# Differential attention, opening: the update of x after the preceding layer norm on GpSimd instead of VectorE

## What is computed

```
# layer 0 ends:
x = layer_norm(ALPHA * x + (1 + gate2) * mlp(h), ln_g, ln_b)
# layer 1 (differential attention) begins:
h = x * (1 + scale1) + shift1
y = diff_attention(h)
x = layer_norm(ALPHA * x + (1 + gate1) * y, ln_g', ln_b')

def layer_norm(x, g, b):
    return (x - mean(x)) * rsqrt(var(x) + eps) * g + b
```

## Time and profile before

| | before |
|---|---|
| median of 3 executions | 1206.44 us (1204.35 to 1206.61) |
| the profiled execution: its time | 1205.25 us |
| the profiled execution: its span | 1203.1 us |
| TensorE busy | 1190.4 us, 99% of the span |
| VectorE busy | 951.6 us, 79% |
| ScalarE busy | 622.0 us, 52% |
| GpSimd busy | 116.9 us, 10% |
| mean granted TensorE clock | 0.998 |

### The profile page before, as it was taken

The page is one execution under the profiler, slowest core; times in us unless marked ns, Lnnn a source line. Parts: engine busy times, 40 slices in busy tenths (PEclk is TensorE's granted clock), DMA queues, the critical chain, the costliest instruction groups (busy, mean ns, idle before and its releaser), DMA issues.

```text
span 1203.1 us, 14725 instructions
## 1 busy us (share of the span) xinstructions
PE 1190.4 (99%) x5734; PEld 976.7 (81%) x5734; DVE 951.6 (79%) x1382; ACT 622.0 (52%) x851; POOL 116.9 (10%) x173
## 2 busy tenths in 40 slices
PE   9999999999999999999999999999999999999997
PEld 7888888888778888888887778888887788888885
DVE  7799868877766689888786668898998878775656
ACT  7445346465774463334465657443446576643441
POOL 2110130221300010000001100000101110000000
PEclk9999999999999999999999999999999999999999
DMA  9999996874655489989467537788857564566540
GB/s 317 336 344 323 311 297 190 286 250 160 178 178 173 152 294 353 311 313 327 162 220 242 162 115 274 269 304 276 313 190 251 165 224 140 177 223 212 191 160 35
DMA packets 148373, 282.71 MB, mean 235 GB/s; under 512 B 6976, under 2 KB 77072, under 8 KB 148304
## 3 DMA queue, kind: packets, MB, share of 16 engines
q1 hardware_dynamic: 127568, 209.73, 52.0%
q0 software_dynamic: 20576, 71.96, 17.9%
q10 hardware_dynamic: 160, 0.07, 0.0%
HBM read 274.61 MB, written 7.13 MB: 234 GB/s over the span
## 4 chain that ended last, share of the span: by engine, by line
PE 92%; DVE 3%; ACT 2%; issue 2%; DMA 0%; SPq 0%; DVEq 0%
PE ps L534 24%; PE ps L536 24%; PE ps L535 24%; PE ps L867 7%; PE ps L866 3%; PE ps L786 2%; PE ps L734 1%; ACT hi_w L1190 1%; PE ps L613 1%; PE ps L1077 1%; PE ps L740 1%; PE ps L1054 1%; PE ps L1056 1%; PE ps L943 1%; ACT area L1507 1%
## 5 line engine op out<-in xcount | busy, mean ns | idle before, releaser
L1706 DVE TENSOR_TENSOR lo_w<-w_raw,hi_w 128x2048 fp32r<-128x2048 f32 x194 | 440.7, 2286 | 61.2 <-ACT hi_w L1190 60.8
L1190 ACT ACTIVATE hi_w<-w_raw 128x2048 fp32r<-128x2048 f32 x195 | 370.0, 1915 | 55.6 <-DMA w_raw<-in_ffn_w_in 20.2
L534 PE MATMUL ps<-hi_w,xT 128*128 128x512 f32 x848 | 338.6, 399 | 0.0
L536 PE MATMUL ps<-lo_w,xT 128*128 128x512 f32 x848 | 330.9, 390 | 0.0
L535 PE MATMUL ps<-hi_w,xT 128*128 128x512 f32 x848 | 330.4, 390 | 0.0
L534 PEld LDWEIGHTS ps<-hi_w,xT 128*128 128x128 f32 x848 | 159.4, 188 | 36.3 <-issue 4.9
L534 PE MATMUL ps<-hi_w,hT_hi 128*128 128x512 f32 x480 | 188.3, 392 | 0.0
L536 PEld LDWEIGHTS ps<-lo_w,xT 128*128 128x128 f32 x848 | 159.2, 188 | 34.3
L536 PE MATMUL ps<-lo_w,hT_hi 128*128 128x512 f32 x480 | 187.0, 389 | 0.0
L535 PE MATMUL ps<-hi_w,hT_lo 128*128 128x512 f32 x480 | 186.8, 389 | 0.0
L535 PEld LDWEIGHTS ps<-hi_w,xT 128*128 128x128 f32 x848 | 159.5, 188 | 30.9
(11 more groups left out here) (324 smaller groups left out, 1169.9 us busy)
## 6 DMA issues: line engine op xcount, KB each, us to landing
w_raw<-in_ffn_w_in SPq DMA_DIRECT2D x86, 512.0 KB
aux<-in_ada_w POOLq DMA_DIRECT2D x34, 1024.0 KB, 7.1
w_raw<-in_mlp_w_up SPq DMA_DIRECT2D x32, 1024.0 KB
w_raw<-in_mlp_w_down SPq DMA_DIRECT2D x32, 1024.0 KB
w_raw<-in_w_mix_in SPq DMA_DIRECT2D x26, 1024.0 KB
w_raw<-in_ffn_w_out SPq DMA_DIRECT2D x22, 1024.0 KB
area<-in_ada_w POOLq DMA_DIRECT2D x14, 1024.0 KB, 6.1
w_raw<-in_moba_w_in SPq DMA_DIRECT2D x12, 1024.0 KB
```

The source lines that it names most:

```text
L534: pe.matmul(dst, lhs_hi, rhs_hi, start=start, stop=False)
L536: return pe.matmul(dst, lhs_hi, rhs_lo, start=False, stop=stop)
L1190: act.activation(hi_w[:, ring_slot(u), :], w_raw[:, ring_slot(u), :], ACT.Copy).then_inc(w_hi, 1)
L1706: vec.tensor_tensor(lo_w[:, ring_slot(u), :], w_raw[:, ring_slot(u), :], hi_w[:, ring_slot(u), :].bitcast(F32), ALU.subtract).then_inc(w_l ...
```

## The change

VectorE's two calls of `x_update` in differential attention go. GpSimd makes x instead, after it has issued the three row loads of the first MLP's layer norm and ahead of the head exchange: it waits for the rows, then for each tile until ScalarE has written its norm, multiplies by g and adds b, both over 1024 columns. VectorE gets three waits on `x_new`: ahead of the copy of turned keys over tile 0 (`heads_out(1)`), ahead of the transpose over tile 1 (`rotate(2)`), and ahead of the first use of x in the attention's own layer norm. The other calls of `x_update`, for the stages S_MOBA and S_DIFF, stay on VectorE.

```diff
-            def ln_summed(t, h):
+            def ln_summed(s, t, h):
                 z = zt[:, t, half_cols(h)]
                 steps.wait(vec)
+                if s == S_DIFF and (t, h) == (0, 0):
+                    vec.wait_ge(x_new, 2 * NT)
...
                     if n in (0, 2):
                         vec.wait_ge(rot_done, hb + 2 + n + 1)
+                        if diff and n == 2:
+                            vec.wait_ge(x_new, 2 * NT)
                         vec.transpose(late_turned[n // 2], buf.rearrange("p t n -> p (t n)")).then_inc(head_turned, 1)
...
                     vec.wait_ge(headT, hb // 2 + n // 2 + 1)
+                    if diff and n == 1:
+                        vec.wait_ge(x_new, NT + 1)
                     vec.tensor_copy(k2T[n // 2], bank(0, 2).rearrange("p (c n) -> p c n", c=4)).then_inc(headT_out, 1)
...
-                    if diff and slot == 6:
-                        x_update(S_MLP1, 1)
...
-                    if slot == 2 and diff:
-                        x_update(S_MLP1, 0)
...
                 if s == S_MLP1:
+                    pool.wait_ge(ld_row, 16 * 3 * (n + 2))
+                    for t in range(NT):
+                        pool.wait_ge(z_quarter, quarter(S_MLP1 - S_MOBA, t, 1))
+                        pool.tensor_tensor(x[:, t, :], zt[:, t, :], row_g, ALU.mult).then_inc(x_scaled, 1)
+                        pool.wait_ge(x_scaled, t + 1)
+                        pool.tensor_tensor(x[:, t, :], x[:, t, :], row_b, ALU.add).then_inc(x_new, 1)
                     heads_exchanged(6, late_turned[0], late_queries[0])
```

More of the change, by code:

```diff
@@ L324, in two_blocks_kernel @@
         ch_act, ch_lo = sem("ch_act"), sem("ch_lo")
-        x_new = sem("x_new")
+        x_new, x_scaled = sem("x_new"), sem("x_scaled")
         xsq_done, rstd_x_done = sem("xsq_done"), sem("rstd_x_done")
@@ L1859, in ln_stats, with ln_moments @@
                 steps.inc(vec.bn_stats(bst[:, t, h, :], zt[:, t, half_cols(h)]))
-            def ln_moments(t, h):
-                ln_summed(t, h)
+            def ln_moments(s, t, h):
+                ln_summed(s, t, h)
                 ln_stats(t, h)
@@ L1881, in ln_part @@
                 ln_gated(s, t, h)
-                ln_moments(t, h)
+                ln_moments(s, t, h)
             def ln_finish(t):
@@ L1907, in after_ln @@
                     vec.wait_ge(third_part_taken, LATE.index(b) + 1)
-                    ln_moments(1, 0)
+                    ln_moments(s, 1, 0)
                     ln_gated(s, 1, 1)
                     late_split(b, 0, 0, 0)
-                    ln_summed(1, 1)
+                    ln_summed(s, 1, 1)
                     late_split(b, 0, 0, 1)
@@ L1926, in after_ln @@
                     quarter_split(b, 0, 1)
-                    ln_moments(1, 1)
+                    ln_moments(s, 1, 1)
                     ln_variance(s, 1)
```

## The result

| kernel | median | lowest to highest | runs |
|---|---|---|---|
| before | 1206.53 us | 1204.35 to 1207.64 | 6 |
| with the change | 1210.92 us | 1209.48 to 1212.73 | 6 |

The ratio is 1.0039, with a 95% interval from 1.0027 to 1.0051: slower by 0.4%, 4.4 us. The prediction said 1210.8 us. The profiled execution with the change took 1209.55 us, with a span of 1207.6 us (before: 1205.25 and 1203.1).

What follows compares the result with a forecast made beforehand. TensorE, busy 1190.4 of 1203.1 us, was taken as the bound. Terms: +5.7 (entry) - 0.9 (keys' gap) - 0.4 (scores' gap) = +4.4 us; on the median of 1206.44, 1210.8 us, range 1207.8 to 1214.2.

Steps and rivals of the forecast that it cites:

- The entry: At the stage's entry GpSimd's instructions hold VectorE's, so TensorE's products come late: +3.1 us first tile, +5.7 us by the second.
- The price of 1024 columns: Each added GpSimd instruction of 128x1024 takes 2.4 us, between 2.26 and 2.56 us.
- Casts: VectorE's casts at the entry wait for GpSimd's whole instruction, like two-operand work; +4.4 us in all, without this +3.6.
- Rival 1: At the entry VectorE's casts are not held by GpSimd: +3.6 us, 1210.0 us; chance 0.12.
- The second tile's sequence: Second tile's entry: cast waits for GpSimd's product until 915.5, subtraction for its addition until 918.05; TensorE 5.7 us later.
- Rival 2: TensorE's clock falls in the entry's two new 3.3 us gaps: +5.8 us, 1212.2, up to 1214 us; chance 0.21.
- The keys' gap: TensorE's 0.90 us wait before the keys' transposes at 933.32 closes: -0.9 us.
- The scores' gap: TensorE's 0.44 us wait for the head exchange before the scores at 940.32 closes: -0.4 us.
- Rival 3: At the entry GpSimd gives way to VectorE, so nothing is late: 0 us, 1206.4 us; chance 0.15.
- Rival 4: GpSimd's first product at the entry carries a set-up that holds the shared path: anything over 1211 us; chance 0.02.

Runs made afterwards that it cites:

- the filled kernel: The change plus eleven extra TensorE matmuls ahead of each tile's entry products, into a bank nobody reads; 1209.61 us, ratio 1.0046 to the kernel before.
- tile 1 alone: The change with GpSimd updating only the second tile (tile 1) and VectorE updating tile 0 at its old place; 1210.12 us.
- tile 0 alone: The change with GpSimd updating only the first tile (tile 0) and VectorE updating tile 1 at its old place; 1208.36 us.
- the kernel with one product there: The kernel before, but GpSimd makes tile 0's product after the second tile's shift, while VectorE idles; VectorE adds b and makes tile 1; 1207.87 us.
- the halves: The change with GpSimd's four instructions over 1024 columns cut into eight over 512; 1211.96 us.
- fills: The kernel before, with GpSimd also writing zeros five times over each tile of x before VectorE makes x; 1207.10 us beside 1205.05.
- the addition alone: The change's four GpSimd instructions added to the kernel before, with VectorE still making x at its old places; 1212.04 us, ratio 1.0045.
- the late kernel: The change with GpSimd's four instructions held until VectorE has split the second tile's chunks; 1212.88 us.
- The removal alone: The kernel before without VectorE's two updates of x, which nobody makes instead; 1204.85 us, ratio 0.9987.

## Why the prediction was right

**The entry.** Predicted +3.1 at the first tile and +5.7 at the second; measured +2.91 and +5.60. The row of L1853 at the kernel's end had the mechanism in it: whoever asks second waits for the end of the other's whole instruction. The removed and the added part, run by themselves, confirm that it is the addition which costs (tail +5.1) and the removal which is worth nothing (+0.1). The Trainium skill (SBUF — State Buffer, "Who interferes with whom") says the same of two-input work and of fp32 casts; the cast's 1.71 us beside a sum and 0.29 beside nothing agree with it.

**The price of 1024 columns.** Between 2.26 and 2.56, taken as 2.4; the second tile's instructions took 2.39 and 2.38. The two of the first tile took 2.75 and 2.67, with their own waits. The line through the figure of the Trainium skill (GPSIMD Engine Reference, section 3.1) is nearly as close; worked out again it gives 2.35, not 2.36.

**Casts.** Taken as held, by an argument and not by a row; they are, as the profile after shows (1.71 and 1.57 us instead of 0.28). Rival 1 is out, and with it its 3.6 us.

**The second tile's sequence was wrong, its end right.** I had the cast asked for at 914.7 (16.37 after the norm) and the subtraction waiting. With the clock's fall it was asked for at 17.93 and waited itself; with the clock held up it was asked for at 16.40, and the sequence is the one predicted. GpSimd's last instruction ends at the same place in both.

**Rival 2** was half right: the clock did fall, in the first gap. It said itself that a fall there is swallowed by the second gap; the filled kernel shows that, with at most 0.25 us between them. In the second gap, of 1.63 us instead of the predicted 3.3, since TensorE came to it late, it did not fall again. Had it, the price could have been 3 us, as with tile 1 alone. That this gap came out short is something that the prediction didn't work out.

**The keys' gap** closed, as predicted. **The scores' gap** did not: -0.4 predicted, +0.22 measured. VectorE began its splits 4.3 us later than before (predicted 4.4). The exchange's second half was issued 40.28 us after the norm, 3.6 later than before, since GpSimd waited 5.64 us for the first half and not the 6.44 of the earlier trace rows. But it landed 6.4 us after its issue, where I had taken over the 5.2 of the earlier trace rows:

```profile
area<-head_scratch POOLq DMA_DIRECT2D x1, 512.0 KB, 6.4
```

This term is mis-sized by 0.6 us. The landing time is not a constant: over the kernels here the exchange took 4.7 to 6.5 us at this place. With tile 0 alone it was issued at the same distance from the norm as with the change, 40.25 us, and landed 4.8 us later, at 45.05; the scores started at 45.18. The other terms measured +5.6 and -0.9. The sum of terms was +4.4; +4.73 is measured at the scores and +4.81 in the tail, inside the bounds of 3.8 to 5.0.

**Rival 3** fell with the first row: L1855 took 2.17 us. GpSimd has no lower rank; wherever both asked here, the one who asked first went first. What is true in it, that GpSimd's work is free in VectorE's idle time, the kernel with one product there shows. **Rival 4** fell too: the first product started 0.16 us after the norm was written and ended 2.26 us after VectorE's split in flight, with no set-up between.

## What to carry to other kernels

Before work is moved from VectorE to an idle GpSimd, look at what VectorE does at the moment at which it would run, not at how idle GpSimd is: every GpSimd instruction tried here that reads SBUF (product, sum, copy) held VectorE's casts and its work with two operands in SBUF until it ended, so that 4.9 us taken off VectorE came back as 4.4 us, nearly all of it standing still on the critical path. The safe places are VectorE's idle stretches and its work with one operand in SBUF that isn't a cast: the moments kept their 0.69 us inside GpSimd's sum, and the product with the gate row, whose other operand is in PSUM, its 0.68 inside GpSimd's product. Whether shorter instructions help, the halves leave open. And a removal is only worth the gap that it closes minus the wait behind it: here the order of VectorE's list alone closed both gaps (1.5 us), which neither half of the change could.

## What the runs showed of the hardware beyond this

**Casts are held by writes too.** GpSimd's fills left two-operand work alone (0.69 and 0.43 us, as ever) but stretched casts of 0.28 us to 0.57 to 0.66, and one of 0.43 to 0.69. So casts depend on more of GpSimd's traffic than two-operand work does.

**The clock comes back after different times.** After gaps of 3.1 to 3.3 us, which look alike, the granted clock stayed at 1.2 GHz for 3.4 us (the change, the addition alone and tile 0 alone) and for 6.8 (tile 1 alone), and for 10.2 around the 6.85 us of the late kernel. What makes the difference I can't tell from these runs. In the kernel in halves two gaps of 1.84 and 0.47 us in the first tile did no harm; in the second tile it fell at 920.9, 1.3 us after a gap of 2.35 us had ended, for 3.4 us. So the length of a gap alone doesn't tell whether the clock falls: with the fills a gap of 3.2 us, at 644 to 647, left it at 1.00.

**Single times of this kernel carry 2 to 3 us from elsewhere.** Kernels that don't differ up to there reached the norm between 898.0 and 901.1 us. Where it was 901.1 (one product in the idle time), the time was lost 250 us earlier, at the preceding attention's first scores. Windows and waits of TensorE in that kernel:

```profile
640.00:650.00 10.00, 8.04 (x35) 6.08 (x34) 3.77 (x10) 5.53 (x11) 1.93 (x4) 0.87 0.88 296
```

```profile
PEld ps L1054 <- issue: 8.1, 16, 2.4
```

In the kernel before the same ten microseconds have 9.25 us of matmuls at a clock of 1.00, and the longest such wait of the weight loads is 1.1 us, not 2.4. There too the scores wait for a head exchange, and its landing time differs from execution to execution: 6.4 us in the kernel before, 7.5 here. The longer wait costs 1.2 us; behind it the clock fell (0.87 in the window above) and was low from 647.6 to 650.8, which costs some 1.6 us more: together the 2.8 us. The kernel in halves (norm at 900.94) goes the same way with a landing time of 6.9 and a fall. In the kernel with the fills (900.66) the exchange took 8.3 us and the wait 3.2; its clock stayed at 1.00, and the longer wait alone makes 2.1 of its 2.3 us. Up to the second tile's products, distances inside the stage repeat to 0.1 us between kernels that don't differ there (14.47 to 14.50 where nothing is held), and the experiments with a single execution rest on them. The scores' distance repeats less well wherever it hangs on the exchange.

**The chain of waits can name a neighbour.** The chain of the kernel before followed the keys' gap to the end of ScalarE's rounding at 929.64, where VectorE's split began at once. It ended just as VectorE's update did (927.24 + 2.4). The removal alone closed the gap: there the second of VectorE's two splits starts at about 927.8, ahead of the end of ScalarE's rounding at 930.17. So it was VectorE's update that held the split; the two ends fell on the same moment.
